# Issuing a row load one step later in the SyncE queue of a decoder layer's attention and convolution stage

## The reference

```python
h = rms(x); proj = h @ w_in            # q | k | v | B | C | xc, 1024 columns each
a = diff_attention(q, k, v)            # 8 heads, ALiBi, QK-norm, then a norm of each head
c = B * causal_conv3(C * xc)           # short convolution, 1024 channels
x = x + concat(a, c) @ w_out
x = x + peer(rms(x))                   # product keys: top 16 experts of 128^2 for 8 heads
# peer: act = gelu(u[expert] . h) * gate; out = sum act * v[expert]
```

## Time and profile before

| what | value |
|---|---|
| time, median of 3 runs | 3037.15 us (3034.65 to 3040.03) |
| profiled execution: its own time / its span | 3034.65 us / 3032.9 us |
| PE busy | 2926.5 us, 96% of the span |
| DVE, POOL, ACT busy | 2329.0, 1516.9, 1015.1 us |
| mean bandwidth of the DMAs | 312 GB/s |
| heads: from about 290 to 626 us | 336 us, 42.2 us per head |

### The profile page before, as it was taken

The page is one execution under the profiler, slowest core; times in us unless marked ns, Lnnn a source line. Parts: engine busy times, 40 slices in busy tenths (PEclk is TensorE's granted clock), DMA queues, the critical chain, the costliest instruction groups (busy, mean ns, idle before and its releaser), DMA issues.

```text
span 3032.9 us, 40948 instructions
## 1 busy us (share of the span) xinstructions
PE 2926.5 (96%) x15249; PEld 2603.8 (86%) x15249; DVE 2329.0 (77%) x3102; ACT 1015.1 (33%) x1245; POOL 1516.9 (50%) x906
## 2 busy tenths in 40 slices
PE   7999999999979999999999999999999999999998
PEld 6888777788879999999999999999997877777887
DVE  5444767754488888888888887798777989988998
ACT  3222333341323233333323332333323333333343
POOL 1000223200035566665656565465856877886772
PEclk9999999999999999999999999999999999999999
DMA  7877687777359998989999898899999999999998
GB/s 263 258 242 220 217 255 232 233 269 250 118 183 317 311 331 289 333 299 316 324 304 341 286 335 285 292 332 339 316 355 371 413 414 413 414 416 415 414 414 361
DMA packets 321777, 947.12 MB, mean 312 GB/s; under 512 B 62485, under 2 KB 179233, under 8 KB 232289
## 3 DMA queue, kind: packets, MB, share of 16 engines
q1 hardware_dynamic: 177040, 475.04, 43.3%
q0 software_dynamic: 107008, 439.75, 40.7%
q10 hardware_dynamic: 37584, 30.43, 3.0%
HBM read 849.56 MB, written 95.55 MB: 312 GB/s over the span
## 4 chain that ended last, share of the span: by engine, by line
PE 66%; DVE 12%; DMA 11%; issue 6%; ACT 4%; ACTq 0%; DVEq 0%; SPq 0%; POOL 0%
PE ps L1695 20%; PE ps L1697 20%; PE ps L1696 20%; DMA v_raw<-in_peer_v 8%; PE ps L1945 4%; DMA wc_raw<-in_w_in 2%; DVE u_row L1569 2%; DVE v_lo L1608 2%; DVE uT_lo L1553 1%; ACT v_hi L1096 1%; DVE uT_lo L1558 1%; ACT uT_hi L1056 1%; PE ps L1795 1%; DVE wq_lo L1427 1%; DVE seg_turned L1215 1%
## 5 line engine op out<-in xcount | busy, mean ns | idle before, releaser
L1695 PE MATMUL ps<-hT_hi,uT_hi 128*128 128x384 f32 x2048 | 701.9, 343 | 29.5 <-DVE uT_lo L1553 26.6
L1697 PE MATMUL ps<-h2T_lo,uT_hi 128*128 128x384 f32 x2048 | 687.2, 336 | 0.0
L1696 PE MATMUL ps<-hT_hi,uT_lo 128*128 128x384 f32 x2048 | 685.9, 335 | 0.0
L759 POOL DMA_INDIRECT gate_grid<-gates,grid_cells x256 | 542.6, 2120 | 121.3 <-issue 76.5
L1695 PE MATMUL ps<-v_hi,a_hi 128*128 128x512 f32 x1024 | 404.2, 395 | 33.2 <-DVE v_lo L1608 31.5
L1695 PEld LDWEIGHTS ps<-hT_hi,uT_hi 128*128 128x128 f32 x2048 | 385.5, 188 | 40.0 <-DVE uT_lo L1553 33.1
L1696 PE MATMUL ps<-v_hi,a_lo 128*128 128x512 f32 x1024 | 401.9, 393 | 0.0
L1697 PE MATMUL ps<-v_lo,a_hi 128*128 128x512 f32 x1024 | 401.5, 392 | 0.0
L1096 ACT ACTIVATE v_hi<-v_raw 128x2048 fp32r<-128x2048 f32 x128 | 245.7, 1919 | 457.5 <-PE ps L1697 344.9
L1696 PEld LDWEIGHTS ps<-hT_hi,uT_lo 128*128 128x128 f32 x2048 | 385.8, 188 | 1.9
L1697 PEld LDWEIGHTS ps<-h2T_lo,uT_hi 128*128 128x128 f32 x2048 | 385.0, 188 | 0.0
(11 more groups left out here) (206 smaller groups left out, 4844.8 us busy)
## 6 DMA issues: line engine op xcount, KB each, us to landing
v_raw<-in_peer_v SPq DMA_DIRECT2D x128, 1024.0 KB, 15.7
u_tile<-in_peer_u SPq DMA_DIRECT2D x88, 1024.0 KB, 7.3
seg_rows<-in_peer_u SPq DMA_DIRECT2D x40, 1024.0 KB, 6.3
u_tile<-uT_all SPq DMA_DIRECT2D x40, 1024.0 KB, 7.3
uT_all<-seg_turned SPq DMA_DIRECT2D x100, 256.0 KB, 6.5
w_raw<-in_w_in SPq DMA_DIRECT2D x24, 1024.0 KB, 6.9
wc_raw<-in_w_in SPq DMA_DIRECT2D x48, 512.0 KB, 7.2
gate_grid<-zeros POOLq DMA_DIRECT2D x16, 1024.0 KB
```

The costliest lines, as they stand in the source:

```text
L759: pool.indirect_dma_start(out=gate_grid, out_offset=bass.IndirectOffsetOnAxis(ap=grid_cells[:, d, col:col + 1], axis=0), in_=gates[:, 2 + ...
L1695: mm(out, a_hi, b_hi, start=first, stop=False)
L1696: mm(out, a_lo, b_hi, start=False, stop=False)
L1697: return mm(out, a_hi, b_lo, start=False, stop=last)
```

## The change

```diff
             with sp.Fori(0, CT - 1) as j:
                 for p in range(PIECES):
                     sp.wait_ge(wc_ready, PIECES * j + p + 1)
                     conv_piece(j + (p + 2) // PIECES, (p + 2) % PIECES)
-                    if p in (2, 5):
+                    if p in (3, 5):
                         next_rows(2 * j + (TURNED_QKV + 3 + p // 5))
```

## The result

The changed kernel takes 3073.16 us (median of 4 runs, 3070.95 to 3074.99) against 3038.59 us for the kernel before on the same chip: ratio 1.0114, 95% interval 1.0101 to 1.0129, so 34.6 us slower. I had forecast 3053, 15.5 us slower, with 3067 as the upper end: the direction was right, the size was not. The profiled execution has a span of 3074.1 us, against 3032.9 before, so these two lie 41.2 us apart.

A forecast was written before the change was run, and what follows sets the result against it. It took a closed ring of PE, DVE, ACT and piece 4's DMA to bound the heads. Six heads at 2.6 less 0.1 us plus 0.5 in head 0 gave 15.5 us more: 3053 us, range 3040 to 3067.

The forecast's parts named there:

- What bounds the heads: Heads: a closed ring of PE, DVE, ACT and piece 4's DMA; PE waits only at `turn_a(0)`, 9.4 us in all.
- Step 1: SP's queue: the rows go out behind piece 5, 5.4 us later than now, and the waits moved with them are already met.
- Step 2: Queue ahead of the rows: piece 5 lands 10.5 us after issue, as in the last head; 12.6 is the other end.
- the sum: Whole kernel: six heads at 2.6 less 0.1 us, plus 0.5 in head 0, 15.5 us slower.
- Step 3: Landing of the rows: 2.6 us behind piece 5, which is 5.0 us after DVE wants them.
- Step 4: From DVE's first transposes to PE's `conv(2)`: 4.65 us behind the rows' landing, so 2.6 us of new idle PE a head.
- the break-even: Rows landing by 396.3 in the trace cost nothing; each us beyond costs a us per head.
- Step 5: Rest of the head: shifts by the same 2.6 us, no price; uncovered, `apply_v(3)` would wait up to 3.4 us.
- Step 6: Wait of `turn_a(0)`: piece 4 lands slightly sooner without the rows behind it, a gain of 0.1 us per head.
- The clock: PE at half clock for 3.42 us after the new idle time: 10 us in six heads, 3063; not in the total.
- The dearer rival: Heads: piece 5 takes 12.6 us, rows 3.2 more, PE idles 5.2 us in six heads: 3068 us; chance 0.20.

The follow-up runs named there:

- Experiments 9 to 12: Kernel before, POOL's second-tile stores moved behind the `b_sb` store: with DVE's transposes moved 3039.24 us; alone 3031.80, repeated 3032.97; with ACT's `aT` copy earlier 3026.77.
- Experiment 1: Changed kernel with the rows issued at the same late step, but ahead of piece 5 in the queue and not behind it: 3041.71 us.
- Experiments 2 and 4: Changed kernel with POOL's zeros written ahead of the heads: all 16 MB, 3058.32 us; half of them, 3047.57 us in a single execution.
- Experiment 8: Changed kernel with DVE's first two transposes of the tile moved to the other two, behind `combined(1)`: 3052.65 us.
- experiment 4: Changed kernel with 1 MB of zeros per head and not 2, the other 8 MB written ahead of the heads: 3047.57 us, single execution.
- experiments 5 and 6: Changed kernel with extra matmuls ahead of the wait of `turn_a(1)`: 18 in every head, 3076.81 us; 12 in all but head 0, 3073.18 us.

## Why the prediction was wrong

- *What bounds the heads* (the ring of PE, DVE, ACT and piece 4): right. Experiments 9 to 12 shortened piece 4 and the wait of `turn_a(0)` went.
- *Step 1, the issue* 5.4 us later and the waits met: right (6.1 us lie between piece 4 and the rows, 0.7 before). Experiment 1 gives 6.5 us of the 37 to the lateness with the rows ahead of piece 5; there DVE still waits 2.0 to 3.3 us a head. I had no price for the lateness by itself.
- *Step 2, piece 5 lands in 10.5 us*: this is the term that failed first. It took 12.7 us in head 2, and 12.3 to 13.3 in heads 1 to 5; only head 6, with 10.7, came as forecast. I argued that part of the 12.6 of the earlier trace rows was the rows ahead of it, and took the last head as the model. But piece 5 took 12.5 to 12.8 us before the change with the rows ahead of it, and no less without. Experiments 2 and 4 show that the zeros set the landing. (In the earlier trace rows q1 also held piece 0 of the next head, issued at 390.48, and not only piece 5; both are pieces of the same kind.) With 12.7 and my own steps 3 and 4 the sum would have been 2.2 us a head higher, about 3066.
- *Step 3, the rows 2.6 us behind the piece*: right, 2.5.
- *Step 4, 4.65 us from the landing to `conv(2)`, and a us per head for each us beyond the break-even*: right, 4.5. PE's new idle time was 4.6 us in head 2 and not 2.6, by the error of step 2; PE's idle time in the heads grew by 24.4 us, where the sum had 15.5. Experiment 8 confirms the path through `biased(2)` and `combined(1)`.
- *Step 5, the rest of the head at no price*: right for heads 1 to 6 of the changed kernel. Where PE ran at full clock, in experiments 1, 4, 5 and 6, `apply_v(3)` waits, 4.7 us in experiment 1 and 5.9 in experiment 4 over the six heads. The step had named this wait, with up to 3.4 us a head.
- *Step 6, the gain of 0.1 us*: the wait of `turn_a(0)` fell from some 1.15 to some 0.85 us. The stores, not the rows, slow piece 4: shown by the runs with the stores moved (3.8 and 3.9 us).
- *The clock*: this is the second term that failed, and counted in PE's own time the larger: it stood at nothing and came to 12.6 us, where the idle time was 8.9 us over the sum's 15.5. I had it in a rival and at no price in the sum, and my 2.6 us lay between a wait that had left the clock alone and one that had not. It came in all six heads, also behind the 2.26 us of head 6, so the two waits of the earlier trace rows did not separate the cases; even the forecast's own idle time gave no ground for leaving it out. PE was busy 12.6 us more for the same work; what of this a full clock would give back in time is open (experiments 5 and 6). The Trainium skill ("TensorE: Matmul & The Clock Gate", section on the HAM clock gate) says that the clock goes from 2.4 to 1.2 GHz when the engine has been idle, and the trace agrees: 0.50 in each of the six stretches. My reason against it, that two transposes break up the idle time, did not hold: they come at its end (413.74).
- *The dearer rival* was the case, but for its sizes: the rows landed 2.5 and not 3.2 us behind the piece, and PE waited 24.8 us at `turn_a(1)` in the six heads, not 31. I set its two halves, late piece 5 and half clock, side by side as two forms with a price each. Both came at once.

What stays open: why piece 5 lands in 10.7 and 10.6 us in the last two heads with the same zeros in flight, why the same zeros cost 23 us ahead of the heads, and how much of the 37 us the slower clock alone costs.

## What to carry to other kernels

What a DMA costs can hang on what is ahead of it in its queue and on what else is in flight more than on its own size: here 0.7 us of issue time and one place in the queue made 30 us. Before moving an issue, read the landing of its new predecessor in exactly that place of the loop, and take the measured landing, not one corrected by reasoning. When the sum gives TensorE an idle stretch near one that has already halved its clock in the same trace, price both together, and do not read a safe length of wait out of two examples.

## What the runs showed of the hardware

- Small packets fall behind large ones: with both queues busy they moved about as many packets each, but 0.19 against 1.40 MB. The landing of a 512 KB piece went from 5.4 to 7.9 to 12.7 us with 0, 1 and 2 MB of zeros of the other queue beside it, while the 1 MB of rows, issued just ahead of the piece in experiment 1, took 10.7.
- PE waits of 2.3 to 5.0 us came in all six heads with 3.4 or 6.8 us at 1.2 GHz; with 18 matmuls in their place the clock stayed at 2.4 GHz. The length of the wait alone does not tell: 1.84 us had such a stretch behind it and 2.12 us in the same trace had none (experiment 8).
- The slow stretches made PE busy 12.6 us longer for the same work. With most of them gone, in the run with 12 matmuls, the heads were 4.5 us shorter, and another wait had appeared; the run with 18 gives no upper bound, since its matmuls delay PE themselves.
